# A hybrid decoder step on one core: the cache copies split and moved into the retrieval stage, and the last layer norm rewritten

## The reference, cut to what matters

```python
# per group of tokens
h = layer_norm(ALPHA * x + mix, ln1_g, ln1_b)
f = peer_ffn(h, ...)                         # 8 retrieval heads, top 16 of 128 x 128 experts
y = layer_norm(ALPHA * h + f, ln2_g, ln2_b)  # mean and variance over 1024 columns

# sample group, for each of the three cache windows
k_all = jnp.concatenate([buf[:, :, 0], k[:, :, gi]], axis=1)
v_all = jnp.concatenate([buf[:, :, 1], v[:, :, gi]], axis=1)
kv_s[gi].append(jnp.stack([k_all[:, n_all - n_prev:], v_all[:, n_all - n_prev:]], axis=2))
```

## Time and profile before

| | us |
|---|---|
| median of 3 runs | 4828.28 |
| the three runs | 4797.03, 4830.7, 4828.28 |
| the profiled execution | 4800.55 |
| its span | 4799.0 |

### The profile page before, as it was taken

The page is one execution under the profiler, slowest core; times in us unless marked ns, Lnnn a source line. Parts: engine busy times, 40 slices in busy tenths (PEclk is TensorE's granted clock), DMA queues, the critical chain, the costliest instruction groups (busy, mean ns, idle before and its releaser), DMA issues. The chain is left out here.

```text
span 4799.0 us, 64513 instructions
## 1 busy us (share of the span) xinstructions
PE 3962.5 (83%) x24889; PEld 3686.0 (77%) x24889; DVE 3043.2 (63%) x5862; ACT 1179.5 (25%) x2121; POOL 1759.1 (37%) x1228
## 2 busy tenths in 40 slices
PE   7897979798999897798066489888888888888882
PEld 7796969657999896687055488888888888888882
DVE  3332323212222234399888699989998999999984
ACT  1212121311111101143289122222222222222221
POOL 0000000000000002377500566666766666666644
PEclk8787879899999999888589699999999999999996
DMA  5433332252111244110024899999999999999973
GB/s 154 152 99 122 108 113 65 78 218 73 59 60 60 85 130 141 56 31 10 0 124 193 333 359 357 355 350 362 360 355 358 348 359 359 356 356 354 358 271 112
DMA packets 470701, 982.63 MB, mean 205 GB/s; under 512 B 49022, under 2 KB 267518, under 8 KB 467427
## 3 DMA queue, kind: packets, MB, share of 16 engines
q0 software_dynamic: 156704, 619.52, 34.6%
q1 hardware_dynamic: 312578, 355.11, 21.8%
q10 hardware_dynamic: 1152, 4.46, 0.2%
HBM read 901.43 MB, written 131.28 MB: 215 GB/s over the span
## 5 line engine op out<-in xcount | busy, mean ns | idle before, releaser
L1879 POOL DMA_INDIRECT u_row<-in_peer_u_dram,eid x512 | 785.1, 1533 | 703.1 <-DVE dots L1938 417.7
L59 PE MATMUL e_ps<-coef_h,v_h 128*128 128x288 f32 x2048 | 661.3, 323 | 243.6 <-DVE v_l L1907 199.4
L59 PE MATMUL e_ps<-hBh,u_h 128*128 128x288 f32 x2048 | 607.4, 297 | 62.8 <-DVE u_l L1900 62.8
L1954 DVE SCALAR_TENSOR_TENSOR f_row<-v_row,g_coef,f_row 128x1024 f32<-128x1024 f32 x508 | 650.9, 1281 | 6.1 <-DMA v_row<-in_peer_v_dram,eid 5.6
L1885 POOL DMA_INDIRECT v_row<-in_peer_v_dram,eid x512 | 573.1, 1119 | 197.4 <-issue 154.2
L59 PEld LDWEIGHTS e_ps<-coef_h,v_h 128*128 128x128 f32 x2048 | 414.8, 203 | 298.1 <-DVE v_l L1907 244.9
L60 PE MATMUL e_ps<-coef_l,v_h 128*128 128x288 f32 x2048 | 634.4, 310 | 0.0
L61 PE MATMUL e_ps<-coef_h,v_l 128*128 128x288 f32 x2048 | 632.1, 309 | 0.0
L1938 DVE CUSTOM_DVE_ANT_0 u_row<-u_row,h_row 128x1024 f32<-128x1024 f32 x512 | 620.9, 1214 | 10.1 <-DMA u_row<-in_peer_u_dram,eid 10.0
L61 PE MATMUL e_ps<-hBh,u_l 128*128 128x288 f32 x2048 | 607.0, 296 | 0.0
L60 PE MATMUL e_ps<-hBl,u_h 128*128 128x288 f32 x2048 | 606.9, 296 | 0.0
(11 more groups left out here) (282 smaller groups left out, 8469.9 us busy)
## 6 DMA issues: line engine op xcount, KB each, us to landing
u_raw<-in_peer_uT_dram SPq DMA_DIRECT2D x128, 512.0 KB, 9.0
v_raw<-in_peer_vQ_dram SPq DMA_DIRECT2D x256, 256.0 KB, 8.5
s_g<-gate_block SPq DMA_DIRECT2D x9, 4096.0 KB, 11.2
x_gate<-s_g SPq DMA_DIRECT2D x64, 576.0 KB
out_o_kv_sample_dram<-in_cache_kv_w_dram POOLq DMA_DIRECT2D x2, 16256.0 KB, 94.6
c_raw<-in_w_in_dram SPq DMA_DIRECT2D x40, 512.0 KB, 3.8
w_raw<-in_w_in_dram SPq DMA_DIRECT2D x96, 192.0 KB, 3.7
cache_v<-in_cache_vS_dram SPq DMA_DIRECT2D x8, 2304.0 KB
```

The source lines that it names most:

```text
L59: pe.matmul(out, lh, rh, start=first, stop=False)
L1879: pool.indirect_dma_start(urow[:, r % RING], None, io["peer_u"][0], bass.IndirectOffsetOnAxis(ap=eid[:, r:r + 1], axis=0)).then_inc(urow_i ...
L1954: dve.scalar_tensor_tensor(out=f, in0=vrow[:, r % RING], scalar=coef[:, s % 2, x:x + 1], in1=f, op0=ALU.mult, op1=ALU.add).then_inc(weighe ...
```

## The change

The four copies of `prompt_attn` become eight pieces, one issued by POOL at the start of each head's `look_up`. The loop of ACT and POOL over the heads is written out, since each piece has its own address. `ln2_out` is written anew: the tiles run in the order 4 to 8, 0 to 3; every tile has its own place in SBUF, so that all loads are issued at once; PE makes ALPHA * h + f in PSUM (h times a scaled identity, plus f times the identity, or `acc` times the identity); DVE reads statistics from PSUM and does scale, gain and bias in two instructions; ACT takes the root and issues the stores, and nothing waits for them but the end. POOL has no part in it. The final wait counts eight copies instead of four.

```diff
@@ prompt_attn, POOL @@
             for s in range(SP):
-                pool.wait_ge(w_lo_done, s * 6 + 6)
-                for g, a, b in ((0, 0, 120), (1, 0, 504)) if s == 0 else ((2, (s - 1) * 508, s * 508),) if s < 3 else ():
-                    pool.dma_start(...).then_inc(k["cache_moved"], 16)
                 pool.wait_ge(at_done, 2 * (s + 1))
@@ retrieve @@
+    COPIES = [(0, 0, 120)] + [(1, 168 * i, 168 * (i + 1)) for i in range(3)] + [(2, 254 * i, 254 * (i + 1)) for i in range(4)]
...
-            with eng.Fori(0, (HEADS - 4) // 2) as q:
-                for p in range(2):
-                    query(q * 2 + (p + 2), p, True)
-                    choose(q * 2 + p, p)
+            for i in range(2, HEADS - 2):
+                query(i, i % 2, True)
+                choose(i - 2, i % 2)
...
             def look_up(h, p):
-
+                g, a, b = COPIES[h]
+                pool.dma_start(io[f"o_kv{g}_sample"][0, :, a:b].rearrange("b r w s2 e -> b (r w s2 e)"),
+                               io[("cache_kv_w128", "cache_kv_w512", "cache_kv_w2048")[g]][0, :, DS + a:DS + b]
+                               .rearrange("b r w s2 e -> b (r w s2 e)")).then_inc(k["cache_moved"], 16)
                 pool.wait_ge(pos_ready, h + 1)
@@ ln2_out, new @@
+    ORDER = tuple(range(GTILES, NT)) + tuple(range(GTILES))
+    NY = 4
...
+            for i, t in enumerate(ORDER):                       # SP
+                n = rows_of(t)
+                sp.dma_start(H[:n, t], io["s_h"][t * P:t * P + n]).then_inc(h_in[t], 16)
                 if t < GTILES:
+                    sp.dma_start(F[:, t], io["s_f"][t * P:(t + 1) * P]).then_inc(h_in[t], 16)
+                if i == 0:
+                    sp.dma_start(gain[:], io["ln2_g"].to_broadcast([P, D])).then_inc(consts, 16)
+                    sp.dma_start(bias[:], io["ln2_b"].to_broadcast([P, D])).then_inc(consts, 16)
...
+            for i, t in enumerate(ORDER):                       # PE
+                n = rows_of(t)
+                if i >= NY:
+                    pe.wait_ge(centred, i - NY + 1)
+                pe.wait_ge(h_in[t], 32 if t < GTILES else 16)
+                for a in range(2):
+                    cols = slice(a * 512, (a + 1) * 512)
+                    pe.matmul(ps[:n, i % NY, cols], scaled_id[:n, :n], H[:n, t, cols], start=True, stop=False)
+                    if t < GTILES:
+                        m = pe.matmul(ps[:n, i % NY, cols], k["ident"][:], F[:, t, cols], start=False, stop=True)
+                    else:
+                        for j in range(4 * a, 4 * a + 4):
+                            m = pe.matmul(ps[:n, i % NY, j * P:(j + 1) * P], k["acc"][:, j, t * P - TA:t * P - TA + n],
+                                          k["ident"][:], start=False, stop=(j % 4 == 3))
+                m.then_inc(y_ready, 1)
...
+            def stats(i):                                       # DVE
+                n, x = rows_of(ORDER[i]), i % 2
+                dve.wait_ge(y_ready, i + 1)
+                for a in range(2):
+                    dve.bn_stats(st[:n, x, 6 * a:6 * a + 6], ps[:n, i % NY, 512 * a:512 * (a + 1)])
+                dve.drain()
+                dve.bn_aggr(mv[:n, x], st[:n, x]).then_inc(var_ready, 1)
+
+            def finish(i):
+                t, x = ORDER[i], i % 2
+                n = rows_of(t)
+                dve.wait_ge(std_ready, i + 1)
+                dve.reciprocal(rstd[:n, x:x + 1], std[:n, x:x + 1])
+                dve.scalar_tensor_tensor(out=H[:n, t], in0=ps[:n, i % NY], scalar=mv[:n, x, 0:1], in1=gain[:n],
+                                         op0=ALU.subtract, op1=ALU.mult).then_inc(centred, 1)
+                dve.drain()
+                dve.scalar_tensor_tensor(out=H[:n, t], in0=H[:n, t], scalar=rstd[:n, x:x + 1], in1=bias[:n],
+                                         op0=ALU.mult, op1=ALU.add).then_inc(done, 1)
+
+            stats(0)
+            dve.wait_ge(consts, 32)
+            for i in range(NT):
+                if i + 1 < NT:
+                    stats(i + 1)
+                finish(i)
...
+            def store(i):                                       # ACT, behind root(i + 1)
+                ...
+                act.wait_ge(done, i + 1)
+                act.dma_start(dst, H[:rows_of(t), t]).then_inc(y_out, 16)
@@ program @@
-                act.wait_ge(k["cache_moved"], 16 * (NG + 1))
+                act.wait_ge(k["cache_moved"], 16 * HEADS)
```

More of the change, by code:

```diff
@@ L2043, in ln2_out, with sb @@
 def ln2_out(nc, io, k):
+    ORDER = tuple(range(GTILES, NT)) + tuple(range(GTILES))
+    NY = 4
     with ExitStack() as c:
+        def sb(n, s):
+            return c.enter_context(nc.sbuf_tensor(n, s, F32))
         def sem(n):
             return nc.alloc_semaphore(n)
-        N = Norm(nc, c, "n2", io["ln2_g"], io["ln2_b"])
-        stage = c.enter_context(nc.sbuf_tensor("f_stage", [P, 2, KD, P], F32))
-        frow = c.enter_context(nc.sbuf_tensor("f_in_row", [P, 2, D], F32))
-        ps = c.enter_context(nc.psum_tensor("f_ps", [P, 2, D], F32))
-        h_in = [sem(f"h_in{x}") for x in range(2)]
-        staged = sem("staged")
-        f_ready = sem("f_ready")
-        y_out = [sem(f"y_out{x}") for x in range(2)]
-        y_stored = sem("y_stored")
+        H, F = sb("f_h", [P, NT, D]), sb("f_rows", [P, GTILES, D])
+        gain, bias, eps = sb("n2_gain", [P, D]), sb("n2_bias", [P, D]), sb("n2_eps", [P, 1])
+        scaled_id = sb("f_alpha", [P, P])
+        st, mv = sb("n2_st", [P, 2, 12]), sb("n2_mv", [P, 2, 2])
+        std, rstd = sb("n2_std", [P, 2]), sb("n2_rstd", [P, 2])
+        ps = c.enter_context(nc.psum_tensor("f_ps", [P, NY, D], F32))
+        h_in = [sem(f"f_h_in{t}") for t in range(NT)]
+        consts, alpha_ready = sem("n2_consts"), sem("f_alpha_ready")
+        y_ready, var_ready, std_ready = sem("f_y_ready"), sem("n2_var_ready"), sem("n2_std_ready")
+        centred, done, y_out = sem("n2_centred"), sem("n2_done"), sem("y_out")
         block = c.enter_context(nc.Block())
@@ new lines, in _ @@
+        @block.tensor
+        def _(pe):
+            pe.wait_ge(alpha_ready, 1)
+            for i, t in enumerate(ORDER):
[13 more added lines that the diff above has]
+                m.then_inc(y_ready, 1)
@@ new lines, in _ @@
+        @block.vector
+        def _(dve):
+            dve.memset(eps[:], EPS)
+            dve.tensor_scalar(scaled_id[:], k["ident"][:], ALPHA, None, ALU.mult).then_inc(alpha_ready, 1)
+            def stats(i):
[21 more added lines that the diff above has]
+                finish(i)
@@ L2073, in _ @@
         @block.scalar
         def _(act):
-            act.wait_ge(N.eps_ready, 1)
-            def step(t, x, n):
-                if t >= GTILES:
-                    if t >= GTILES + 2:
-                        act.wait_ge(f_ready, t - GTILES - 1)
-                    act.activation(stage[:, x, :, :n], k["acc"][:, :, t * P - TA:t * P - TA + n], ACT.Copy).then_inc(staged, 1)
-                N.root(act, t, x, n)
-            over_tiles(act, step)
-        @block.vector
-        def _(dve):
-            N.start(dve)
-            def step(t, x, n):
-                dve.wait_ge(y_stored, t + 1)
-                dve.wait_ge(h_in[x], 16 * loaded(t))
-                if t >= GTILES:
-                    dve.wait_ge(f_ready, t - GTILES + 1)
-                N.stats(dve, x, n, ps[:n, x] if t >= GTILES else frow[:n, x])
-                N.scale(dve, t, x, n)
-            over_tiles(dve, step)
@@ L2113, in _, with root @@
-        @block.tensor
-        def _(pe):
-            for t in range(GTILES, NT):
-                x, n = t % 2, rows_of(t)
-                pe.wait_ge(staged, t - GTILES + 1)
-                pe.wait_ge(N.summed, t + 1)
-                for j in range(KD):
-                    m = pe.transpose(ps[:n, x, j * P:(j + 1) * P], stage[:, x, j, :n], k["ident"][:])
-                m.then_inc(f_ready, 1)
+            def root(i):
+                n, x = rows_of(ORDER[i]), i % 2
+                act.wait_ge(var_ready, i + 1)
+                act.activation(std[:n, x:x + 1], mv[:n, x, 1:2], ACT.Sqrt, bias=eps[:n]).then_inc(std_ready, 1)
@@ L2124, in program @@
+            def store(i):
+                t = ORDER[i]
+                dst = io["o_y_prompt"][0, t * P:(t + 1) * P] if t < PT else io["o_y_sample"].rearrange("b s d -> (b s) d")
+                act.wait_ge(done, i + 1)
+                act.dma_start(dst, H[:rows_of(t), t]).then_inc(y_out, 16)
+            root(0)
+            for i in range(NT):
+                if i + 1 < NT:
+                    root(i + 1)
+                store(i)
+            act.wait_ge(y_out, 16 * NT)
 def program(nc, io, phases=99):
```

24 lines of the change are left out of this document (removed).

## The result

The changed kernel takes 4847.99 us (median of 20 runs, 4803.82 to 4861.35). The kernel before, run beside it, takes 4799.42 (4784.33 to 4833.16). The ratio is 1.007, 95% interval 1.0043 to 1.0096: slower by 0.7%, where 4712, 2.4% under the 4828.28 of then, was forecast. Against this profile's execution of before (4800.55 us) the profiled one of after (4846.72 us) is 46 us longer, so the two traces show what the medians show. The medians lie 1.0% apart and the means (4807.7 and 4841.3) 0.7%, since the runs of each kernel fall into two groups. Group against group it is 22 to 23 us: the lower ones have means of 4791.5 and 4813.7, the upper ones 4827.5 and 4850.4, and more runs of the changed kernel are in the upper one. What the groups may be comes further down.

The account below looks back on a forecast made before the run. Bounds: weight loads stuck behind copies and PE's half clock in `prompt_attn`, DVE in `retrieve`, POOL in series with stores in `ln2_out`. 4800.55 - 62 - 8 - 36 + 1 = 4696; median 4696 to 4730, taken 4712; range 4655 to 4760.

Parts of the forecast that it names:

- The copies enter `retrieve`: Terms for copies moved into `retrieve`; the second item prices POOL's eight issues of 0.69 us, 5.5 us altogether, at 0.
- the three signs: Signs of being wrong: POOL issues lasting microseconds, ACT waiting for query weights, PE waiting longer than DVE in `ln2_out`.
- The third rival: In `retrieve`, POOL is held at each piece's issue, about 30 us mean to decide for slower; 4882 us, chance 0.04.
- 16 us to spare a head: In `retrieve`, POOL's idle time per head, (365 - 238) / 8, taken to absorb part of each hold.
- The copies in time: In `retrieve`, landing times: 254-row pieces 47 us, 168-row pieces 31, the first 22 to 29.
- Query weights: In `retrieve`, SP's query weight loads sharing engines with the copies cost 0, up to 5 us if a pair is late.
- The table for `build_gates`: The table that `build_gates` waits for may land late: 1 us taken, at most 17.
- A term that I put at 0: In `retrieve`, writing the loop out changes nothing that DVE waits for: 0.
- `prompt_attn`, -62 and -8: Copies leaving `prompt_attn` remove weight waits and second-half waits, 62 us; 8 more from no clock fall before slot 0's split.
- `ln2_out`, -36: The rewritten last stage, paced by DVE at 4.5 us a tile, saves 36 us; 14.5 at half clock, 40 if warm.
- the second rival: In `ln2_out`, PE at half clock holds the last stage: 4712 + 21.5 = 4733 us, chance 0.07.
- The first rival: In `prompt_attn`, PE's clock survives the split, 26.4 us a slot: one slot 4686, all three 4633; chance 0.12.

Follow-up runs that it names:

- the kernel with the semaphore: The changed kernel with POOL's drain between product and half sum of each look-up replaced by a semaphore; 4747.76 us, ratio 0.9865.
- the probe: The kernel before, with a memset, a drain and a second memset on POOL behind the copies in `prompt_attn`; 4820.01 us beside 4821.95.
- the reversed order: The kernel with the semaphore plus spare products, more of them in units 1 to 9, and the eight copies issued large ones first; 4647.54 us, ratio 0.9661.
- spare products: Thrown-away PE products filling its pauses, first added to the kernel with the semaphore at the junction and units 10 and 11; 4649.77 us, ratio 0.9659.

## Why the prediction was wrong

**The step that failed.** It is the second item under "The copies enter `retrieve`": POOL's issue "lies in front of a wait that POOL has to sit through anyway ...: 0". The 0.69 us were right (0.65), and the wait in front of which it lies is there once the drain is gone (8.3 to 19.6 us in six of the heads with the semaphore). What I left out is that the copy stays outstanding when POOL goes on, and that the look-up has a drain between the product and the half sum. I followed the engine's queue past the issue but didn't list each instruction behind it that waits for the engine to be empty. The runs put 92.5 us on it (549.1 with the drain, 456.6 with a semaphore), and the probe shows the mechanism alone, 89 us against 0.2. In `prompt_attn`, where the trace of before has the same copies, POOL has no drain, so no row of that trace showed it. Of the three signs by which the text would have known itself wrong (POOL's issues in microseconds, ACT waiting for query weights, PE waiting in the last stage) none came; the one that did was the forecast's own, DVE near 94% in `retrieve`, which was 74%.

**The third rival** had the consequence right and the place wrong. POOL was held once a piece, the look-up was late and DVE behind it. But it was held at the drain, not at the issue, 21.4 us a piece (5.35 to 33.11, 171.6 in all for the eight), less than the 30 us from which it was to decide for slower, and the stage still lost 110. "16 us to spare a head" was too generous: it is a mean of POOL's idle time, and part of that comes where POOL waits on ACT or DVE and can't take work forward. It had 0.04, for reasons that spoke only of the issue. The rule of the Trainium skill that the prediction cites for this rival (SBUF — State Buffer, section "SBUF: two separate sides") is not borne out by the trace: with DVE 74% busy in the stage, issues took 0.65 us, and the 8128 KB pieces landed after 48.9 us, near the 47 worked out from `prompt_attn`, where DVE was much less busy. With the semaphore, DVE 81% busy (252.11 of 311 us), they landed after 52.8. Which of DVE's instructions here are of the kind that the rule means, no trace shows.

**Other terms of `retrieve`.** The copies in time: 48.9 and 29.3 us measured for 47 and 31. Query weights: in the program's order 0, as said, and the reversed order shows the price where that reason is gone, 71.2 us. The table for `build_gates`, taken as 1 and bounded by 17, was 12.5 late with ACT issuing; with POOL issuing and the semaphore, the block's end waited for the copy instead, 7.8 less 0.4. In the kernel as changed neither came up, since the last piece had landed in the drain. A term that I put at 0 is some 13 us: DVE's waits beside instruction transfers. Whether the written-out loop or the copies' traffic makes them, the runs don't separate. The kernel with the large copies first has both and only two such waits, of 4.3 us each.

**`prompt_attn`, -62 and -8.** The waits went as said: SP's eight loads take 4.36 us, and ACT no longer waits for weights at the split in the units of slots 0 to 2. From one last store of statistics to the next, slot 0 gained 13.4 us, slot 1 17.6 and slot 2 19.6, 50.7 in all; 62 were worked out. The difference is the clock. Slots 1 and 2 lost it at the junction instead of at the split, which costs the units in between too; the 8 us of slot 0 weren't won, for the same reason. The bound of this term (0 to 79 on the gain's side) had no end for that. Which slots lose it at the junction is luck: the kernel with the semaphore has the same `prompt_attn`, and in its profile slots 0 and 2 lost the clock there, slot 1 only behind the split (0.79 from 395 to 405), as the forecast assumed, and slot 3 not at all. Then slot 3, warm in the profile of before, fell in that of after: 38.0 us given back (its own time is 179.9 us before and 217.9 after), where the text had 34 for such a fall and set it aside as a matter of chance. It does seem to come in about half or more of the runs. Before's 20 runs lie in two groups, 11 at 4784 to 4802 and 9 at 4822 to 4833, and after's in 5 at 4804 to 4822 and 15 at 4839 to 4861. That fits one slot more or less with a full clock, and the mean granted clock of each run bears it out: 0.888 to 0.892 in after's five lower runs, 0.879 to 0.887 in its other fifteen. Runs of before taken beside the kernel with the semaphore show the same, six at 4773 to 4790 us with 0.891 to 0.895 and eleven at 4813 to 4827 with 0.879 to 0.888. By my estimate, slot 3's 48.4 us at 1.00 (863.62 to 912.03 before) turned into 85.9 at 0.50 (813.48 to 899.34 after) take the mean from 0.889 to 0.881. Which slot it is in a given run, only the profiled ones show. Nor do the runs say why the fall at the junction comes more often with the copies gone, if it does: in the two other profiles that have the copies in `prompt_attn`, those of the new `ln2_out` alone and of the drain shown by itself, slot 3 fell too (53.4 us).

**`ln2_out`, -36.** Measured -41.5, 1.5 us beyond the upper bound of 40. DVE takes 4.07 us a tile (4815.71 to 4819.77 from one finish to the next) in place of 4.5. PE takes 3.5 us a tile for tiles 4 to 7, where 3.7 were counted, and 3.4 for tiles 0 to 3. The count was right in time and not in make-up: in tiles 4 to 7 each half has one 512-column product and four of 128 columns, two records each, and takes 1.75 us. The groups of the kernel after, shapes apart, have these sixteen short records for each of the four tiles:

```profile
L2091 PE MATMUL f_ps<-ident,acc 128*128 128x128 f32 x64 | 9.7, 303 | 0.0
```

So PE is hidden behind DVE by only half a microsecond a tile. PE was at full clock, so the second rival fell. **The first rival**, the clock survives the split, is also false: in the six profiles without spare products and without the copies in `prompt_attn`, slots 0 to 2 all took 53.4 us from L263 to L267. Only spare products kept the clock past the split.

**The sum.** 4800.55 - 12.7 - 5.3 + 110.3 - 0.8 - 4.2 - 41.5 = 4846.4, the profiled run of after (4846.72). How far the rest of my sum held shows in the profiled run of the kernel with the semaphore, 4711.54, where slot 3 was at full clock as in the profile that I summed against: 4696 was the forecast on that footing. Its differences from my terms are `prompt_attn` +16.3 (-53.7 for -70), `retrieve` +16.8 (17.8 for 1), `ln2_out` -6.0 (-42.0 for -36), and -11.6 in the stages between, for which I had nothing and have no cause: 15.5 in all. Its median, 4747.76, lies 36 us higher, about slot 3's fall. The upper end of the range, 4760, is short of what the text puts into it: 4730, 21.5 for the half clock and 16 for the late table make 4767.5. The measured 4848 lies beyond either.

## What to carry to other kernels

Before an asynchronous transfer is moved in front of other work, look for every drain and every end of a block behind it on the same engine: on POOL each waits until the transfer has landed, so the price of the issue is the landing time less the work in between. Between two instructions of the same engine a semaphore does what the drain does here, without that wait, and a queue of another engine is the other way out. A gap in the trace with "issue" as its releaser, that ends where a transfer lands, is the sign to look for.

## What the runs showed of the hardware that I had not expected

- A drain on POOL holds until POOL's own transfers have landed: 89.44, 89.28 and 88.47 us behind 16 MB copies, 0.20 with none outstanding. Transfers issued by ACT didn't hold POOL's drain (0.6 us over the stage), and ACT's own drain behind its issue showed no wait.
- The end of a block did the same on POOL (the next stage 52.6 us behind the last issue, 7.8 us of it exposed), and not on ACT (32.9 us behind it).
- Beside copies, with 169 GB/s moved in the stretch 2055 to 2366 of the semaphore's kernel, DVE's waits with instruction packets in them were 10.5 and 9.0 us (6.82 + 3.63 and 6.42 + 2.58) in the two passes, where the kernel before has 3.2 and 3.3. The loop was written out as well, and with the large copies first they were 4.3 and 4.3, so the cause is open.
- A 64 KB table took 14.1 us to land behind an 8128 KB copy issued by ACT, 1.7 with none beside it.
- In `prompt_attn` the granted clock fell to 1.2 GHz at the start of the light units though PE was busy 4.16 and 4.51 us of the two stretches of 5 us around it in slot 0 (160 to 170), and 3.67 of 5 just ahead of it in slots 1 to 3. The kernel before kept the clock with the same 3.67 in slot 3. Once down, PE was busy without a gap from 815 to 900 and didn't get it back. Four spare products in each of nine units, besides those at the junction and the split, kept it at 2.4 GHz in all four slots, in each of the three profiles that have them.
